# Two stacked transformer blocks on one core: taking out TensorE's products that nobody reads

## The reference

```
h = x                                                   # (512, 1024)
for layer 0:  h += even_layer(rmsnorm(h))               # pooling + 6-head differential attention
              h += sigmoid(h @ ple_w_gate) * (p @ ple_w_proj)
for layer 1:  h += odd_layer(rmsnorm(h))                # 4-head latent attention + gated delta rule
              h += sigmoid(h @ ple_w_gate) * (p @ ple_w_proj)
h = concat(meta_tokens, h)                              # 528 rows
for layer 0:  h += fox_attention(rms_norm(h))           # 16 heads, causal, forget gates
              h += hier_moe(rms_norm(h))                # top 2 of 32 experts, within one of 4 groups
for layer 1:  h += hgrn2_recurrence(rms_norm(h))        # 8 heads, chunked scan
              h += hier_moe(rms_norm(h))
return h[16:]
```

## Time and profile before

| | us |
|---|---|
| median of three runs | 2584.37 |
| lowest, highest | 2577.43, 2586.96 |
| the profiled execution, its own time | 2573.32 |
| its span, first to last instruction | 2571.4 |
| TensorE busy (matmul) | 2436.0, 95% of the span |
| TensorE busy with L378 | 35.7 |
| VectorE, ScalarE, GpSimd busy | 1095.7, 631.7, 646.1 |
| mean granted clock of TensorE | 0.987 of full |

### The profile page before, as it was taken

One profiled execution on the slowest core, in us unless ns is written; L12 is line 12 of the kernel. 1 busy time (PEld: TensorE's weight loads), 2 busy tenths in 40 slices (PEclk: granted clock), 3 DMA queues, 4 the chain that ended last, 5 costly groups with the idle time before them and its releaser, 6 DMA issues. The chain is left out here.

```text
span 2571.4 us, 38187 instructions
## 1 busy us (share of the span) xinstructions
PE 2436.0 (95%) x15328; PEld 1353.3 (53%) x15328; DVE 1095.7 (43%) x2115; ACT 631.7 (25%) x1461; POOL 646.1 (25%) x753
## 2 busy tenths in 40 slices
PE   8998999899989999999999999989999899999998
PEld 5554446756544444555445445458556454454543
DVE  4636554564255554765212111263667542111213
ACT  2216213433211221732011000032456121000100
POOL 1733343462124241440000000020345200000001
PEclk9999999999999999999999999989999999999999
DMA  5521022110120411154999999961011469999998
GB/s 193 191 96 58 32 96 66 54 37 3 36 82 10 157 66 67 50 217 192 394 425 426 426 425 426 424 209 66 35 35 35 166 249 425 426 426 426 427 426 359
DMA packets 119467, 537.28 MB, mean 209 GB/s; under 512 B 24734, under 2 KB 41118, under 8 KB 86560
## 3 DMA queue, kind: packets, MB, share of 16 engines
q1 hardware_dynamic: 111440, 516.23, 50.2%
q0 software_dynamic: 7888, 19.14, 2.0%
HBM read 509.89 MB, written 33.06 MB: 211 GB/s over the span
## 5 line engine op out<-in xcount | busy, mean ns | idle before, releaser
L4045 PE MATMUL psum<-arena,hidden_T 128*64 128x512 f32 x1376 | 303.0, 592 | 0.0
L4057 PE MATMUL psum<-weight_ring,hidden_T 128*64 128x512 f32 x1024 | 239.0, 609 | 18.4 <-DMA weight_ring<-in_moe_w_down 17.5
L4023 PEld LDWEIGHTS psum<-hidden_T,arena 128*128 128x128 f32 x1832 | 212.4, 192 | 40.6 <-issue 40.6
L4023 PE MATMUL psum<-hidden_T,arena 128*128 128x128 f32 x1832 | 226.3, 278 | 0.0
L4045 PEld LDWEIGHTS psum<-arena,hidden_T 128*64 128x64 f32 x1376 | 100.5, 137 | 193.3 <-issue 193.2
L4303 ACT ACTIVATE hidden_T<-psum 128x256 f32<-128x256 f32 x64 | 24.5, 383 | 701.4 <-PE psum L4045 701.4
L4045 PE MATMUL psum<-weight_ring,hidden_T 128*64 128x512 f32 x672 | 149.2, 594 | 0.0
L4039 DVE TENSOR_TENSOR hidden_T<-psum,norm_gains 128x512 f32<-128x512 f32 x64 | 43.8, 690 | 242.0 <-PE psum L4045 153.0
L4057 PEld LDWEIGHTS psum<-weight_ring,hidden_T 128*64 128x64 f32 x1024 | 70.9, 139 | 143.0 <-issue 134.3
L4093 POOL DMA_INDIRECT expert_rows_out<-hidden_T,small x30 | 29.7, 990 | 456.6 <-DVE hidden_T L4405 402.9
L4093 POOL DMA_INDIRECT expert_rows_out<-arena,small x30 | 29.8, 993 | 386.4 <-DVE arena L4405 345.2
(11 more groups left out here) (673 smaller groups left out, 4443.5 us busy)
## 6 DMA issues: line engine op xcount, KB each, us to landing
arena<-in_moe_w_up SPq DMA_DIRECT2D x86, 2048.0 KB, 22.3
weight_ring<-in_moe_w_down SPq DMA_DIRECT2D x64, 2048.0 KB, 21.2
weight_ring<-in_moe_w_up SPq DMA_DIRECT2D x42, 2048.0 KB, 21.7
weight_ring<-in_hg_w_in SPq DMA_DIRECT2D x8, 2048.0 KB, 10.9
weight_ring<-in_ev_w_in SPq DMA_DIRECT2D x8, 1536.0 KB, 9.1
weight_ring<-in_fox_w_in SPq DMA_DIRECT2D x6, 2048.0 KB, 12.1
weight_ring<-in_od_w_in SPq DMA_DIRECT2D x5, 2048.0 KB, 7.9
weight_ring<-in_ple_w_gate SPq DMA_DIRECT2D x4, 2048.0 KB, 8.7
```

The lines of the kernel that those rows point to most:

```text
L4023: last = nc.tensor.matmul(g.psum[:, c // 4, (c % 4) * P:(c % 4 + 1) * P], keep[:, i, c * P:(c + 1) * P], row[:, i, :], start=i == 0, stop= ...
L4045: last = nc.tensor.matmul(g.psum[64 * q:64 * q + 64, 2 + n, :].rearrange("p (s c) -> p s c", s=2), xT[:, k // 4, k % 4, ROWS * n:ROWS * n ...
L4057: last = nc.tensor.matmul(g.psum[64 * q:64 * q + 64, 6 + n, :], aT[:, k % 2, 64 * (k // 2):64 * (k // 2) + 64], down[b][:, k, 512 * q:512 ...
```

## The change

All calls of `hold` are taken out, with the helper itself; in `stage_hg` the wrapper `hold_free` goes as well, with the two waits that it made before its products (they guard the bank that its products wrote). The products of the loading stage (L322) stay. No other instruction, wait, buffer or DMA is changed, none is moved, and the lines of the changed kernel are numbered from 5 to 23 lower behind the edits.

```diff
-def hold(g, bank, times):
-
-    keep_busy(g.nc, bank, g.c("identity"), g.const[:, 0:512], times)
...
@@ stage_ple
                 if s == steps[-1]:
                     pe.wait_ge(*multiplied.at(len(blocks) - 1))
-                    hold(g, bank(4 + len(blocks) % 2), 4)
@@ stage_even_attention
                 for q, k in pieces.get(j, []):
                     project(q, k)
-                if j == 3:
-                    hold(g, g.psum[:, 7, :], 2)
                 if 3 <= j < N + 3:
                     turn(j - 3)
@@ stage_delta
             for n in (NCH - 2, NCH - 1):
-                hold(g, g.psum[:, 3, :], 2)
                 turn_rows(n)
@@ stage_fox_attention
-                if (kind, p) == ("tail", 0):
-                    hold(g, g.psum[:, 4, :], 1)
                 pe.wait_ge(*normed.at(j + 1))
...
             for j in range(N + 4):
-                if j == 3:
-                    hold(g, g.psum[:, 7, :], 1)
                 if j < N:
                     scores(j)
-                if j == 3:
-                    hold(g, g.psum[:, 7, :], 2)
                 if 3 <= j < N + 3:
                     turn(j - 3)
@@ stage_route
         turn_back(0)
         turn_back(1)
 
-        hold(g, g.psum[:, 3, :], 8)
         pe.wait_ge(*counted.at(1))
@@ stage_hg
-            def hold_free(times):
-                for signal, n in order[-2:]:
-                    pe.wait_ge(*signal.at(n))
-                hold(g, bank(0), times)
-
             def finish(h):
-                if h == HG - 1:
-                    hold_free(3)
                 pe.wait_ge(*gated.at(h + 1))
                 if h + 2 < HG:
                     pe.wait_ge(*kplaced.at(2 * (h + 2) + 2))
                 elif h:
                     pe.wait_ge(*moved.at(h))
```

## The result

The changed kernel takes 2587.3 us in the median of 19 runs (2582.9 to 2594.9). The kernel before, run beside it, takes 2578.3 us; the ratio on record is 1.0038, with an interval of 1.0030 to 1.0047: 9 us slower. (One execution of the kernel before, of 4200.8 us, is left out of the ratio and the means as disturbed.) Forecast was +14.3 us. The time of 2598.7 came from adding that to a median of three runs that lay 6 us above the median of 19. Against the 2573.3 us of the profiled execution the same sum gave 2587.6; that this lies 0.3 us from the measured median is luck, because a difference 5 us too large was added to an execution 5 us quicker than the median.

What follows compares the result with a forecast made beforehand. TensorE's work at its granted clock, plus waits in its chain, was taken as the bound. Dips 14.4 + hand-over 2.0 + attention 2.6 - gains 4.7 = +14.3 us on 2584.4 gave 2598.7 us, range 2584 to 2605.

Steps and rivals of the forecast that it cites:

- the mechanism and the sign: Without the products, TensorE's clock falls to half in and behind the waits they filled; slower by 14.3 us.
- The rival of the still waits: Only waits with TensorE standing still lower the clock: routings, second embedding stage, recurrence; +6.2 us, 2590.6 us, chance 0.13.
- The rival that the clock holds: Work left in the waits keeps the clock up, so only the gains stay; -4.7 us, 2579.7 us, chance 0.05.
- the last rival: With stage changes behind them all dips are doubled; +21.9 us, 2606.3 us, chance 0.08.
- The gains: Time by which products outlast their waits: first embedding 0.8, second routing 0.5, recurrence 3.2, attention 0.2; 4.7 us in all.
- The second rival: Dips come beside other work: experts' stream makes up late starts, attention stages have slack; +6.4 us, 2590.8 us, chance 0.07.
- the price of a dip, 6 x 2.4 us: Half-clock stretches on dense work behind two embedding stages, delta, two routings and recurrence: 2.4 us each, 14.4 us.
- the slower hand-over: Transposes at half clock: 0.5 us in each embedding stage, 0.25 at each of four other places; 2.0 us.
- In the embedding, delta and recurrence places a change of stage follows, which everything waits for: Claim that TensorE's delay at these places reaches the program's end, so their dips count in full.
- None of these places has a lower clock now: Claim that, apart from the recurrence, the clock is full at the products' places in the kernel before.
- The attention stages' 2.4 us: Dips at 1.3 us for each of two attention stages, 2.6, less a gain of 0.2 us.
- 35 to 40 us more at half clock: Expected sign in the changed kernel's profile: mean granted TensorE clock 0.979 to 0.981, down from 0.987.

Runs made afterwards that it cites:

- e4: Kernel before without the recurrence stage's three products alone; 2572.5 us against 2576.8, ratio 0.9981, means differ by -4.2 us.
- f4: Kernel before without the recurrence's three products, run once more; 2574.0 us against 2578.0, ratio 0.9986, means differ by -3.8 us.
- e6: Kernel before with twelve products for eight in both routings; 2585.0 us against 2578.0, ratio 1.0024, means differ by +6.9 us.
- d1: Kernel before without the recurrence's three products and the eight of both routings; 2577.7 us against 2576.8, ratio 1.0001.
- d3: Kernel before without the recurrence's products and those of both attention stages; 2581.2 us against 2576.8, ratio 1.0012.
- e5: Kernel before with two more unread products in each of the four output stages; 2580.3 us against 2576.9, ratio 1.0012.
- f5: Kernel before with six products for four in both embedding stages; 2575.3 us against 2578.0, ratio 0.9994.
- e1: Changed kernel with the eight products of both routings put back; 2586.0 us against 2576.8 for the kernel before, ratio 1.0036.
- e2: Changed kernel with both embedding stages' and the delta stage's products put back; 2587.0 us against 2576.8 for the kernel before, ratio 1.0048.
- f2: Changed kernel with both embedding stages' and the delta stage's products put back, once more; 2590.0 us against 2578.0, ratio 1.0039.
- a2: Changed kernel run again without further edits; 2586.4 us against 2576.9 for the kernel before, ratio 1.0032.
- e3: Changed kernel with the products of both attention stages put back; 2584.3 us against 2576.8 for the kernel before, ratio 1.0031.
- d2: Kernel before without the products of the recurrence, both embedding stages and the delta stage; 2578.5 us against 2576.8, ratio 1.0003.
- e8: Kernel before with half of the products in the embedding stages, delta stage and routings; 2580.7 us against 2576.8, ratio 1.0018.
- e7: Kernel before with the recurrence's three products moved ahead of the last but one transposes and made five; 2572.8 us against 2576.9, ratio 0.9992.
- b2: Kernel before, unchanged, profiled once more in one execution; 2584.1 us.

## Why the prediction was off

**Right: the mechanism and the sign.** The products that nobody reads keep the clock up at their places in more than half of the profiles that have them; without them it fell at each of the places named, in every profile. The rival of the still waits (+6.2 us) is nearer to the measured 9.1 than the forecast is, but by its places it is wrong: it had no dip in the first embedding stage and none in the attention stages, and in the first embedding stage and at the start of the first attention stage the clock fell in every profile without the products, in the changed kernel with TensorE never still for over 2.55 us there. The rival that the clock holds is refuted by every profile. The longer dips of the last rival came (6.8 and 10.2 us at most places, 13.7 in the first routing), but not at their price of 21.9 us. The gains were right where they were large: the recurrence's 3.2 us shows as 2.8 in its timeline, and e4 and f4 have it as a gain in time. That a late start of the experts counts in full is shown by e6. The second rival, that the routings' dips are hidden beside other work, is refuted by it: what the first routing adds to the shift stays.

**Wrong: the price of a dip, 6 x 2.4 us.** "2.4 us for each of six places" took each dip as if all of TensorE's lateness went into the time of the program, and as if the kernel before had none there. With the slower hand-over and the gains these six places were forecast at +11.9 us; in the traces they are worth 2.5. By groups:

| term | forecast | in time, from e4's side (d1 to d3) | all profiles |
|---|---|---|---|
| two routings | +4.8 | +4.5 | +2.8 |
| stage ends (two embedding stages, delta) | +7.65 | +5.2 | +2.3 |
| recurrence | -0.55 | -4.0 (e4, f4) | -2.6 |
| two attention stages | +2.4 | +7.3 | +6.6 |
| sum | +14.3 | +13.0 | +9.1 |
| all dropped at once, in time | | +9.1, +9.2 | |

Two steps failed in it. The first: "In the embedding, delta and recurrence places a change of stage follows, which everything waits for". That is where the forecast asked whether the delay reaches the end, and it didn't look through the stage behind for the first row in which TensorE waits. Delta's +2.65 measured 1.1, the second embedding stage's +2.9 nothing, and the recurrence is 2.0 to 3.4 us better than forecast, for one reason: behind each of them TensorE waits for another engine (1.44 and 1.45 us for VectorE in the output stages, 1.29 for ScalarE and 1.28 for VectorE behind the second embedding stage), and a late TensorE only fills that wait. e5 and f5 show it with products at full clock. The second: "None of these places has a lower clock now". That was true of the one execution whose profile was read. In others the clock falls in the first embedding stage and in both routings with the products in place, and so the removal adds 1.7 us there and not 2.9, and 2.3 and 0.5 in the routings and not 3.1 and 1.7. The time of d1 puts the routings at 4.5 us, that of e1 at 0.2, each with an error of some 1.8; the traces' 2.8 lies between them.

**Wrong the other way: the attention stages, and how long the clock stays down.** The attention stages' 2.4 us measured 6.6 in the traces, 7.3 by d3 and 6.0 by a fit of four costs to all the kernels that drop or keep a group. 2.7 of it is at the start of the first, where 1.3 was taken, and 3.0 in the tail of the second, where the forecast has "too short to matter". The products of the tail and those of the stage's start were only dropped together, so which of them the tail misses isn't shown. "35 to 40 us more at half clock" were 62 to 64. A dip at full price costs 0.5 us for each us at half clock, and in place of that 13.4 us of cost over 62 to 64 us is 0.21. Part of it falls into waits, where it costs nothing, and part into the slack above. (The Trainium skill, "TensorE: Matmul & The Clock Gate", section on HAM oscillation, takes half of the throttled time as the penalty; here the measurement decides, and it is less than half of that.) The errors went against each other, so that the total is nearer than its terms.

**Also off: the base.** The median of the three runs, to which the difference was added, was 2584.4; 19 executions have 2578.3, and the means of the comparisons below it 2576.7 to 2577.9. That alone is 6 of the 11.4 us between the forecast and the median measured; the other 5 are the terms.

**What stays open.** In time the costs don't add up, and the fit says so with more than the scatter of the means: with recurrence -2.8, routings +5.3, stage ends +3.3 and attention +6.0 (each mean weighted by its own scatter and that of the kernel before beside it) it misses the means of eight kernels by a chi-square of 36 at 4 degrees of freedom. The clearest case is e2 and f2. Two things stand in the profiles and may be part of it. In the tail of the second attention stage, among many small products, TensorE's issue stands still for some 2.4 us, here in the changed kernel:

```profile
1127.89 1.18 PE L3372 MATMUL psum<-arena 128*32 128x64 f32 x49
1131.44 0.78 PE L3372 MATMUL psum<-arena 128*32 128x64 f32 x31 [2.36 <-issue]
```

It is in the profiles of the changed kernel, a2, e2, e3, d2, d3 and e8 (2.3 to 2.8 us), and in none of the other eleven; e3, d2 and e8 have attention's products, so it doesn't hang on those. And a2, e2, f2, e7, b2 and d2 lose 2 to 3.5 us between 600 and 700 us, in the delta stage, at stretches of half clock; such stretches stand there in sixteen of the eighteen profiles, mostly without that loss. One profile for each kernel can't tell whether either belongs to the kernel or to the execution. That wasn't tried further.

## What to carry to other kernels

Products that keep the clock up earn their place only where they end before the wait does, and enough of them must stand there: here the three that outlasted their wait by 3 us cost 4 us and taking out these alone beats both kernels, while taking out the rest costs 13 us, and half of them don't do. They are no full cover: in the routings and the first embedding stage the clock fell in four to six of some ten profiles with all of them in place. One profile is one execution: before a place is called free of dips, read it in several. When a delay is priced, look in the stage behind for the first row in which the engine waits for another: up to that wait the delay costs nothing. Add a forecast difference to the mean of many executions, and price a dip by rows behind it, since a us at half clock cost 0.2 to 0.4 us here and not 0.5.

## What the runs showed of the hardware

- The clock's dips aren't tied to the program alone: behind the same work in the first embedding stage (1.09 of 3.40 us busy, then 3.40 of 3.40) the granted clock was 0.50 in one execution of the kernel before and 1.00 in another. Executions of one kernel have 51 to 98 us at half clock, and 20 us between the quickest and the slowest.
- Four products in the first routing's wait of 7 us (TensorE idle 3.27 us of it, e8) didn't keep the clock up behind them. Eight, which fill the wait, did: in none of the ten profiles with eight does a dip begin behind them. In e1, e4, e5 and b2 one begins just before them or under them.
- A stream of 80 small products (128x64) stood still for 2.36 us with no wait that the profile names, in the changed kernel; seven of eighteen profiles have such a stop in that tail, of 2.3 to 2.8 us.
